# Token sums of thirteen RMS norms: squares as the stationary operand and a small root chain

## The reference

```python
def rmsnorm(x, g, eps=NORM_EPS):
    x32 = x.astype(jnp.float32)
    y = x32 * lax.rsqrt(jnp.mean(x32 * x32, axis=-1, keepdims=True) + eps)
    return (y * g.astype(jnp.float32)).astype(x.dtype)
...
        x = x + 0.5 * swiglu(rmsnorm(x, norm_g[i, 0]), ffn_w_up[i, 0], ffn_w_down[i, 0])
        h = rmsnorm(x, norm_g[i, 1])
...
        x = x + mix
        x = x + 0.5 * swiglu(rmsnorm(x, norm_g[i, 2]), ffn_w_up[i, 1], ffn_w_down[i, 1])
    return rmsnorm(x, final_norm_g)
```

## Time and profile before

| what | value |
|---|---|
| median of 3 runs | 3937.09 us (3930.63 to 3938.62) |
| profiled execution | 3937.09 us, span 3935.3 us |
| PE busy | 3526.3 us, 90% |
| DVE, ACT, POOL busy | 40%, 34%, 32% |
| sums L494 | 736 matmul records (368 instructions) |
| spreads L506 | 92 records (46 instructions) |
| roots L1106, reciprocals L1568 | 13 each, 9 table loads ahead of the roots |
| granted clock, mean | 0.943 |

### The profile page before, as it was taken

The page is one execution under the profiler, slowest core; times in us unless marked ns, Lnnn a source line. Parts: engine busy times, 40 slices in busy tenths (PEclk is TensorE's granted clock), DMA queues, the critical chain, the costliest instruction groups (busy, mean ns, idle before and its releaser), DMA issues.

```text
span 3935.3 us, 50073 instructions
## 1 busy us (share of the span) xinstructions
PE 3526.3 (90%) x17896; PEld 2817.5 (72%) x17896; DVE 1554.5 (40%) x2356; ACT 1351.0 (34%) x2246; POOL 1245.5 (32%) x683
## 2 busy tenths in 40 slices
PE   6999988999999998887899968899898997679998
PEld 5788766788778876665688847788787886446666
DVE  1322263322232224564322233665566665434443
ACT  3322233322232224444322233334333333324443
POOL 4344432344434442221244413333343333100001
PEclk9999999999999999998999978999999998779999
DMA  4333221333233321111122211110010101100001
GB/s 159 125 112 112 92 79 54 107 123 112 94 109 123 112 93 61 55 56 40 59 96 96 96 52 38 38 37 33 32 37 32 43 32 59 33 6 22 21 21 38
DMA packets 72964, 269.76 MB, mean 69 GB/s; under 512 B 8096, under 2 KB 8096, under 8 KB 72096
## 3 DMA queue, kind: packets, MB, share of 16 engines
q1 hardware_dynamic: 64944, 236.14, 17.9%
q10 hardware_dynamic: 7920, 32.25, 2.2%
HBM read 264.16 MB, written 4.19 MB: 68 GB/s over the span
## 4 chain that ended last, share of the span: by engine, by line
issue 46%; PE 28%; POOL 17%; DVE 6%; ACT 2%; POOLq 1%; ACTq 0%; DVEq 0%
POOL wl L392 15%; PE ps L469 13%; PE ps L916 2%; PE ps L898 2%; PE ps L482 1%; PE ps L925 1%; PE ps L484 1%; PE ps L483 1%; PE ps L785 1%; PE ps L798 1%; PE ps L835 1%; POOL xs L417 1%; DVE rstd L1786 1%; PE ps L899 1%; POOL xe L422 1%
## 5 line engine op out<-in xcount | busy, mean ns | idle before, releaser
L392 POOL TENSOR_TENSOR wl<-raw,wh 128x1024 fp32r<-128x1024 f32 x438 | 1055.8, 2411 | 2559.2 <-ACT wh L1092 2559.2
L1092 ACT ACTIVATE wh<-raw 128x1024 fp32r<-128x1024 f32 x438 | 463.2, 1057 | 1200.3 <-PE ps L469 537.9
L469 PE MATMUL ps<-hh,wh 128*128 128x512 f32 (+1 forms) x1856 | 739.1, 398 | 30.8 <-DVE hl L1581 30.1
L469 PE MATMUL ps<-hh,wl 128*128 128x512 f32 (+1 forms) x1856 | 721.8, 389 | 0.0
L469 PE MATMUL ps<-hl,wh 128*128 128x512 f32 (+1 forms) x1856 | 717.7, 387 | 0.0
L469 PEld LDWEIGHTS ps<-hh,wh 128*128 128x128 f32 x1856 | 355.2, 191 | 137.4 <-issue 49.0
L469 PEld LDWEIGHTS ps<-hh,wl 128*128 128x128 f32 x1856 | 355.0, 191 | 75.9
L469 PEld LDWEIGHTS ps<-hl,wh 128*128 128x128 f32 x1856 | 355.7, 192 | 70.0 <-issue 1.7
L482 PE MATMUL ps<-fh,wh 128*128 128x512 f32 x768 | 307.0, 400 | 4.9 <-DVE fl L1613 3.0
L484 PE MATMUL ps<-fh,wl 128*128 128x512 f32 x768 | 301.3, 392 | 0.0
L483 PE MATMUL ps<-fl,wh 128*128 128x512 f32 x768 | 299.5, 390 | 0.0
(11 more groups left out here) (313 smaller groups left out, 5337.5 us busy)
## 6 DMA issues: line engine op xcount, KB each, us to landing
raw<-stream_dram SPq DMA_DIRECT2D x438, 512.0 KB, 3.2
modw<-mod_dram ACTq DMA_DIRECT2D x48, 512.0 KB, 3.7
x<-xT_dram SPq DMA_DIRECT2D x1, 2048.0 KB, 8.1
side<-ctxT_dram ACTq DMA_DIRECT2D x2, 1024.0 KB, 7.5
park_dram<-x ACTq DMA_DIRECT2D x1, 2048.0 KB, 8.5
x<-park_dram ACTq DMA_DIRECT2D x1, 2048.0 KB, 8.0
out_dram<-x SPq DMA_DIRECT2D x8, 256.0 KB, 2.2
side<-memT_dram SPq DMA_DIRECT2D x1, 1024.0 KB, 5.0
```

The source lines that it names most:

```text
L392: nc.gpsimd.tensor_tensor(wl[:, u % RING, :], raw[:, u % RAW, :], wh[:, u % RING, :].bitcast(FP32), ALU.subtract).then_inc(s_lo, 1)
L469: last = nc.tensor.matmul(bank, a[:, s, w], b[:, k, c0:c1], start=(k == 0 and a is wh and b is hi), stop=(k == KD - 1 and a is wl))
L1092: nc.scalar.activation(wh[:, u % RING, :], raw[:, u % RAW, :], ACT.Copy).then_inc(s_hi, 1)
```

## The change

The operands of the sum are swapped: the 128 squares of a chunk are the stationary operand and one column of ones moves. Each sum goes to a column of its own in `B[7]` (8c + k), on 128 partitions, and is not accumulated. DVE then adds the eight columns of each chunk with a new tensor_reduce, and a new semaphore `ss_ready` tells ACT, whose root is over 128x4 (or 128x2) values instead of 128x128. The reciprocal is as small. The spread takes a column of `rstd`, broadcast, as stationary and the identity as moving operand, with the same number of matmuls. A memset of `rt` falls away.

```diff
@@ norm_sum (PE)
-                last = nc.tensor.matmul(B[7][32 * c:32 * c + 32, 0:P], ones[:, 0:32], sqr[:, k % 2, chunk(c)],
-                                        start=(k == 0), stop=(k == KD - 1))
+                last = nc.tensor.matmul(B[7][:, KD * c + k:KD * c + k + 1], sqr[:, k % 2, chunk(c)], ones[:, 0:1],
+                                        start=True, stop=True)
@@ norm_spread (PE)
-                last = nc.tensor.matmul(B[6][:, chunk(c)], ident[:, 32 * c:32 * c + 1].to_broadcast([P, P]), rstd[:, 0:P],
-                                        start=True, stop=True)
+                last = nc.tensor.matmul(B[6][:, chunk(c)], rstd[:, c:c + 1].to_broadcast([P, P]), ident, start=True, stop=True)
@@ root (ACT)
-            act.wait_ge(sq_used, 8 * n + 8)
-            rows = slice(0, width // P * 32)
-            nc.scalar.activation(rt[rows, 0:P], B[7][rows, 0:P], ACT.Sqrt, bias=eps6[rows, 0:1],
+            act.wait_ge(ss_ready, n + 1)
+            nc.scalar.activation(rt[:, 0:width // P], rstd[:, KD:KD + width // P], ACT.Sqrt, bias=eps6[:, 0:1],
                                  scale=1.0 / D).then_inc(rt_ready, 1)
@@ DVE
+        def sums(name, width):
+
+            dve.wait_ge(sq_used, 8 * NORM[name] + 8)
+            nc.vector.tensor_reduce(rstd[:, KD:KD + width // P], B[7][:, 0:width // P * KD].rearrange("p (c k) -> p c k", k=KD),
+                                    AX.X, ALU.add).then_inc(ss_ready, 1)
+
         def reciprocal_root(name, width):
+            sums(name, width)
             dve.wait_ge(rt_ready, NORM[name] + 1)
-            nc.vector.reciprocal(rstd[:, 0:P], rt[:, 0:P]).then_inc(rs_ready, 1)
+            nc.vector.reciprocal(rstd[:, 0:width // P], rt[:, 0:width // P]).then_inc(rs_ready, 1)
             dve.wait_ge(rb_ready, NORM[name] + 1)
...
-        nc.vector.memset(rt[:, 0:P], 1.0)
```

More of the change, by code:

```diff
@@ L281, in build @@
     sq_ready, sq_used, rt_ready = sem("sq_ready"), sem("sq_used"), sem("rt_ready")
-    rs_ready, rb_ready = sem("rs_ready"), sem("rb_ready")
+    ss_ready, rs_ready, rb_ready = sem("ss_ready"), sem("rs_ready"), sem("rb_ready")
     tmp_ready, h_hi, h_ready = sem("tmp_ready"), sem("h_hi"), sem("h_ready")
```

## The result

The kernel after the change takes 3974.8 us (median of 4 runs, 3970.9 to 3976.5) against 3937.5 for the one before (4 runs). The ratio is 1.0097 with a 95% interval of 1.0080 to 1.0114: 37 us, 1%, slower. The forecast was slower by 27 (3964 us, range 3946 to 3972), so the sign was right, the size short by 10, and the result lies 3 us above the upper end of the range. The profiled execution of after has a span of 3972.1 us, 36.8 more than that of before, at a mean granted clock of 0.938 instead of 0.943.

What follows compares the result with a forecast made beforehand. TensorE, busy for 90% of the span, was taken as the bound. The terms, 9.7 - 1.9 + 14.4 + 3.2 - 0.15 + 2.0 = +27 us, on 3937 gave 3964 us, range 3946 to 3972.

Steps and rivals of the forecast that it cites:

- Term 1: Sums inside projection streams, six norms: 1.7 us more in each of four, +0.7 in each of four mixer gaps; together +9.7.
- Terms 3 and 4: Lone sums at half clock: `ffn0` and `lat0` +7.2 us each, +14.4; `mem` and `ctx0` +1.6 each, +3.2.
- terms 2 and 5: Tails (sum 6 to spread) of the six stream norms, -1.9 us; the rest: `lat1` -0.15, `ctx1` 0, `last` +2.0.
- The sums warm the clock: Rival: back-to-back loads in the sums count as activity and raise the clock; +15 us, 3952; chance 0.25.
- The stream hides the loads: Rival: in streams PE takes the squares' loads beneath running matmuls, so stream bursts cost what they did; 3942 us; chance 0.12.
- loads cost the same at half clock: Rival: a pair in the lone sums costs 0.112 us at half clock too; +11 us, 3948; chance 0.05.
- The clock is held: Rival: the clock stays up through the norms, so nine spreads (-7.3 us) and stage starts (-16) run faster; 3929; chance 0.08.

Runs made afterwards that it cites:

- e3: The kernel after the change, but each sum's matmul moves 128 columns of ones instead of one, with overlapping targets: 3949.1 us, ratio 1.0029.
- e5: The kernel after the change, but with root and reciprocal over 128 columns again: 3983.9 us, ratio 1.0118.
- e2: The kernel after the change, but only the seven lone norms have the new sums and small chain, the other six the old ones: 3960.9 us, ratio 1.0060.
- e1: The kernel after the change, but only the six norms summed in projection streams have the new sums and small chain: 3955.5 us, ratio 1.0045.
- e10: The kernel before plus useless 512-column matmuls ahead of sums 6 and 7, before and behind the spread in six stream norms, two in `last`: 3933.2 us, ratio 0.9985.
- e11: The kernel before plus only two useless 512-column matmuls between last sum and spread, in the six stream norms and `last`: 3934.4 us, ratio 0.9991.
- e9: The kernel before, unchanged, executed once more for a second trace: 3936.8 us.

## Why the prediction was right in direction and short in size

| term | predicted | measured in the traces |
|---|---|---|
| 1, sums in streams | +9.7 | +9.7 |
| 2, six tails | -1.9 | +1.4 |
| 3, `ffn0` and `lat0` | +14.4 | +14.6 |
| 4, `mem` and `ctx0` | +3.2 | +2.4 |
| 5, `lat1` | -0.15 | -0.2 |
| 5, `ctx1` | 0 | +0.6 |
| 5, `last` | +2.0 | +5.0 |
| between the norms | not in it | +3.4 |
| sum | +27 | +36.8 |

The measured column is how much later the same PE instruction stands in the trace of after, from one end of a part to the other; the 0.3 us by which a first load comes earlier behind other matmuls is taken off. The rows are rounded one by one.

**Term 1** held in every part: no drain, a single sum +0.35 for 0.34, a pair +1.01 for 1.02, nothing under VectorE's wait, 1.7 in each of four norms and 0.7 in each of four gaps of the mixers. In `e3` the stretch from `pool`'s first load to sum 6 is 28.82 us, as in after (32.27 - 3.46 = 28.81): the pitch of a full-clock burst is that of its loads, whether one column moves or 128.

**Terms 3 and 4**: the unknown half-clock pair, taken as 0.207 from the spread's loads, came as 0.213. It nearly doubles at half clock, as the load record does (333 ns for 185). `mem` gave +0.8 for +1.6: the new norm took the forecast's 7.8 (7.89), but the old one was not like `ctx0`, which stood in for both. In `mem` the old root waited for a table load that ends at 17.48, so the old norm took 6.87 and not 6.18, and the new, longer sums cover that load. (The load rule of the Trainium skill, TensorE: Matmul & The Clock Gate, LDWEIGHTS, has one value, columns over 1.2 GHz, and none for the lower clock; by it the half-clock pair would be as short as the full-clock one, and the 0.213 beside 0.112 disagrees.)

**What failed is the size of terms 2 and 5.** The sum of term 2 had "15 x 0.112", and `ctx1` "at full clock: sums and chain cancel, 0"; both took for granted that a stretch at full clock stays there, because the old sums did. `last` was given a fall of the clock, but too late: "some 20 pairs" cold, and of those half, where the trace has the fall at 3952.9 and 36 of 63 pairs at 0.21 behind it: 5.0 instead of 2.0. Together 3.3 + 0.6 + 3.0 = 6.9 of the 9.6 us missing; `mem` takes 0.8 back, and the stretches between the norms hold the rest. That it is mainly the clock `e3` shows: with the same loads, the same chain and only more columns moved, the tails are 2.88, the figure that the forecast's own rows give at full clock, and `last` takes 8.8. So of `last`'s 5.0 the clock has 12.18 - 8.82 = 3.4, and 1.6 stand at full clock, where the forecast had 1.1. The bound "0 and 2.5" for the cold part was no bound: it had the time of the fall built in. `ctx1` is no clean case: at 1.00 it is +0.5 in `e3` and +0.1 in `e5`, so the clock has only a part of its 0.6.

**The rest, +3.4 between the norms**, is not settled. A part is shown by rows: `final`'s spread, at 0.97 in the earlier trace rows, is cold now, 0.8. 3.2 us are in one stretch, from `diff`'s spread to `ffn3`'s first sum, and `pool` to `ffn1` gives 1.9 back. The long stretch reads +4.1 in `e2`, where neither norm was changed, so it is no cost of their sums or chains. But it reads only +0.7 in the second trace of the unchanged kernel, and more in the changed kernels from `e1` to `e5` (+1.4 in `e3`, +5.7 in `e5`), and +1.9 and +2.0 in `e10` and `e11`. Whether it is the wander that `e9` shows elsewhere or something that any change brings about stays open, as does why `diff`, and in `e1` `pool` and `final`, keep the clock through their tails.

**The rivals.** *The sums warm the clock* was wrong for this kernel (0.50 in 13 us of `ffn0` and of `lat0`), and near in its arithmetic: `e3` is that case, +11 measured for +15. *The stream hides the loads* and *loads cost the same at half clock* are excluded by the +0.35 a sum and the 0.213 a pair. *The clock is held*: the opposite happened, and `e10` and `e11` show that its 16 us from the stage starts were not there to win.

## What to carry to other kernels

Read a half-busy or even a gapless PE row together with its granted clock, because a full busy share doesn't tell its level (13.00 of 13.00 us busy at 0.50 here). A full-width fp32 load for one moved column pays for the load and may also lose the clock for what follows. When a forecast's rows come from a stretch at full clock, price the new burst at both levels, unless a trace shows the same burst holding the clock. Where a norm stands in for another, look whether both have a table load in front of the root. Before giving VectorE more elementwise work, look in the trace for how long it takes on two SBUF operands while GpSimdE runs.

## What the runs showed of the hardware that was not expected

- Back-to-back pairs of a 128x128 fp32 load and a matmul of one column show PE as busy for 13.00 of 13.00 us at clock 0.50, with no rise; 16 columns are the same (3974.9 us), and with 128 columns the clock rises within the sums and the kernel takes 3949.1. The Trainium skill (TensorE: Matmul & The Clock Gate, Part 1) ties the clock to how busy PE has been; if that is read as the profile's busy share, these rows disagree.
- At full clock such a burst lets the clock fall under it: in `last` about 3 us after the first sum, with PE busy throughout.
- The pair's pitch is 0.11 us at 1.00 and 0.21 at 0.50, with one column, 16 or 128.
- VectorE's 128x512 fp32 addition of two SBUF operands takes 0.68 us, and 2.36 beside GpSimdE's 128x1024 one.
- Between two executions of the unchanged kernel a norm's sums and chain repeat to 0.01 us, while the clock of a spread (0.97 or 1.78 us for `ffn2`) and the stretches between the norms (3.0 longer, 3.3 shorter) don't.
